# Streaming encoder step on one core: levels two and three of the triangular inverse by one product of 128 columns, token copies moved behind

## The chip, the cores and the metric

One Trainium2 chip, one core of it. The metric is the device time of one execution in microseconds, the median of several runs. Everything is computed in float32 (the large matrix products as a sum of three products of split operands).

## The reference, cut to what matters

The kernel does one inference step of a two-layer trunk on 512 prompt tokens and 64 sample tokens (576 columns together). In each layer a norm and an input projection feed two groups of token mixers; their outputs are projected back, and a convolutional feed-forward part follows. The change touches only the RWKV-7 mixer, whose reference is a scan over tokens:

```
def step(s, inp):
    rt, wt, kt, vt, at, bt = inp
    sa = jnp.einsum('bhvk,bhk->bhv', s, at)
    s = s * wt[:, :, None, :] + sa[..., None] * bt[:, :, None, :] + vt[..., None] * kt[:, :, None, :]
    y = jnp.einsum('bhvk,bhk->bhv', s, rt)
    return s, y
```

There are 8 heads with a 64 by 64 state each. The kernel does the scan in chunks of 64 tokens. Inside a chunk each token depends on the earlier ones through a strictly triangular 64 by 64 matrix L per head, and the kernel needs the inverse of (1 - L). It is built as a product, T = (1 + L)(1 + L^2)(1 + L^4)..., over five levels of squaring. The GLA mixer, a chunked linear attention, runs interleaved with it.

## The kernel before, in words

**Stages.** In each layer come the input projection (dense products, two weight tiles in flight), the chunk loop over nine chunks (one of sample tokens, eight of prompt tokens), the output projection, and two halves of the feed-forward part. `passes` (L643 to L652) issues the dense products. The chunk loop is written out by hand for every engine: each engine has one function per step and calls them in a fixed order in its own loop `for i in range(-1, LAST)`. Turn i of the loop finishes chunk i (state, outputs) and prepares chunk j = i + 1 (its masks, its inverse). Each step waits on semaphores whose counts are named by the lists `PE_F`, `AC_F`, `DV_F`, `PO_F`: `nth(AC_F, n, "L2A")` is the count reached when ScalarE has done that step of chunk n.

**The inverse.** The eight heads stand as two sets, A (`hp` 0) and B (`hp` 1), each with two X and, in each X, two heads on the two halves of the partitions. `DET` is a double buffer in SBUF with three slots of 64 columns for each set and X: slot 0 holds the power L^n, slot 1 the growing inverse T, slot 2 the transposed power. Level k reads buffer (k + 1) % 2 and its results go to buffer k % 2:

- TensorE, `level(j, hp, k)`: for each X and for both heads it multiplies slot 2 by slot 0 (L882: the next power, levels 1 to 3), slot 0 by slot 2 (L885: its transpose, levels 1 to 4), both into the PSUM bank `gr[hp]`, and slot 2 by slot 1 (L888: the product that T grows by, levels 2 to 5) into another PSUM bank, `tk[hp]`. The stationary operand of L882 and L888 is the same, slot 2.
- ScalarE, `copy_powers(j, hp, k)` (L1479, at level 4 L1481): copies the powers from `gr[hp]` to `DET`.
- VectorE, `add_power(j, X, k)` (L2057): adds the product in `tk` to T. It waits for the level on TensorE and for T of the level before. Level k + 1 on TensorE waits for both the copy and the addition.

The banks `tk` also hold, from column 0 to 383, the transposed tokens of the chunk (`tokens(j)`, L861), which ScalarE copies out in one instruction, `copy_tokens(j)` (L1471). So level 2 waits for this copy (name "tok" in `AC_F`). In the loop of ScalarE it stands ahead of the copies of level 1.

**Order around it on TensorE in turn i:** `carried` (L908), `solve_z` (L932), `carried_y` (L920), `gram` (L849, L851), `solve_z1` (L942), `gla_scores` (L997), means, `solve_z2` (L950), `tokens`, level 1 of A and of B, `solve_u` (L958), sums of squares (L670, L671) in some turns, level 2 A and B, `outputs` (L966 to L977), `gla_tokens` (L1006, L1008), level 3 A and B, `post_squares_y` (L670, L671) in some turns, `gla_out` (L1024, L1028), level 4 A and B, `gla_state` (L1038, products of 128 columns), level 5 A and B. In the first turn `turn_state` (L821) stands between level 4 and `gla_state`.

**ScalarE in turn i:** copies of carried terms (L1487, L1494), of Z1 (L1499), roots and mixed outputs of an earlier group in some turns (L1573, L1579, L1588, L1597), `copy_tokens`, the copies of level 1, U (L1499 again), statistics (L1555, L1527, and a logarithm, L1561, for turns with a GLA group), the copies of level 2, statistics, the GLA tokens (L1646), the copies of level 3, a logarithm (L1567) or mixed outputs, the GLA outputs (L1656), the copies of level 4.

**VectorE in turn i:** `add_z` (L2066), masks (L2034, L2036, L2043), `add_rest` (L2082), GLA scores (L2102), statistics and scalings (L2131, L2142, L2149, L2157, L2165, L2171), the additions of level 2, `new_state` (L2095, L2097), `add_y` (L2076), in some turns the low parts of the squares that `post_squares_y` sums (L2142), the additions of levels 3 and 4, `new_gla_state` (L2114, L2116), the additions of level 5.

Of the kernel before, what the change touches and what calls it, by code (L numbers as in the profile page):

```python
# [31 lines left out]
C = 64  # L32
# [76 lines left out]
AC_F = ["tok", "L1A", "L1B", "L2A", "L2B", "L3A", "L3B", "L4A", "L4B"]  # L109
# [31 lines left out]
def program(nc, x_prompt, x_sample, state_gla, state_rwkv, state_rwkv_shift, cache_ffn_conv,  # L141
# [4 lines left out]
    with ExitStack() as ctx:  # L146
# [187 lines left out]
        pe_f, ac_f, dv_f, po_f = sem("pe_f"), sem("ac_f"), sem("dv_f"), sem("po_f")  # L334
# [311 lines left out]
        def _(pe):  # L646
# [80 lines left out]
            for l in range(0, DEPTH):  # L727
# [137 lines left out]
                def level(j, hp, k):  # L865

                    N, d = "AB"[hp], DET[(k + 1) % 2]
                    powers = gr[hp][:, 0:4 * C].rearrange("p (x c t) -> p x c t", x=2, c=2)
                    product = pair3(tk[hp][:, 0:2 * C])
                    if k == 1:  # L870
                        front(dv_f, DV_F, j, "M" + N)
                    else:
                        front(ac_f, AC_F, j, f"L{k - 1}{N}")
                        if k == 2:
                            front(po_f, PO_F, j, "T" + N)
                            front(ac_f, AC_F, j, "tok")
                        else:
                            front(dv_f, DV_F, j, f"L{k - 1}{N}")
                    for X in range(2):
                        for h in HEADS:  # L880
                            if k < 4:
                                mm = e.matmul(powers[h, X, 0], d[h, hp, X, 2], d[h, hp, X, 0], start=True, stop=True)  # L882
                        for h in HEADS:
                            if k < 5:
                                mm = e.matmul(powers[h, X, 1], d[h, hp, X, 0], d[h, hp, X, 2], start=True, stop=True)  # L885
                        for h in HEADS:
                            if k > 1:
                                mm = e.matmul(product[h, X], d[h, hp, X, 2], d[h, hp, X, 1], start=True, stop=True)  # L888
                    mm.then_inc(pe_f, 1)
# [33 lines left out]
                def solve_z(i):  # L923

                    front(ac_f, AC_F, i, "tok")
                    front(dv_f, DV_F, i, "MB")
                    glas(ac_g, AC_G, i, "oE")
                    if i > 0:
                        back(dv_a, DV_A, i - 1, "Y")
                    for n, hp, X, o in solved(zb):  # L930
                        for h in HEADS:
                            mm = e.matmul(o[h], EK[i % 2][h, hp, X, 1, C:2 * C], tok[i % 2][h, X, 2, hp, :],  # L932
                                          start=True, stop=True)
                    mm.then_inc(pe_b, 2 if i == 1 else 1)
# [313 lines left out]
        def _(ac):  # L1248
# [87 lines left out]
            for l in range(0, DEPTH):  # L1336
# [131 lines left out]
                def copy_tokens(j):  # L1468
# [3 lines left out]
                                 PS[1].rearrange("p (x n) -> p x n", x=2)[:, :, 0:6 * C], ACT.Copy).then_inc(ac_f, 1)  # L1472

                def copy_powers(j, hp, k):

                    step(pe_f, PE_F, j, f"L{k}" + "AB"[hp])
                    src = gr[hp][:, 0:4 * C].rearrange("p (x c t) -> p x c t", x=2, c=2)
                    if k < 4:
                        e.activation(DET[k % 2][:, hp, :, 0:3:2, :], src, ACT.Copy).then_inc(ac_f, 1)  # L1479
                    else:  # L1480
                        e.activation(DET[k % 2][:, hp, :, 2, :], src[:, :, 1, :], ACT.Copy).then_inc(ac_f, 1)  # L1481
# [127 lines left out]
                for i in range(-1, LAST):  # L1609
# [18 lines left out]
                    copy_tokens(j)  # L1628
# [11 lines left out]
                    copy_powers(j, 1, 2)  # L1640
                    if i == LAST - 1:
# [6 lines left out]
                    copy_powers(j, 1, 3)  # L1648
                    if i == LAST - 1:
# [81 lines left out]
        def _(dv):  # L1731
# [30 lines left out]
            for l in range(0, DEPTH):  # L1762
# [284 lines left out]
                def add_power(j, X, k):  # L2047
# [7 lines left out]
                    src = pair3(tk[X][:, 0:2 * C])  # L2055
# [316 lines left out]
```

## Time and profile before

| what | value |
|---|---|
| median of 3 runs | 1640.76 us (1640.54 to 1641.64) |
| the profiled execution, its own time | 1642.36 us |
| its span, first to last instruction | 1640.6 us |
| granted TensorE clock, mean | 0.996 |
| TensorE busy with matmuls | 1610.7 us, 98% of the span |
| VectorE, ScalarE, GpSimd busy | 955.0, 681.9, 593.6 us |
| chunk loops with their tails | about 211 to 357 us and 1012 to 1157 us of the span |

In the profile one float32 matmul of the code stands as two MATMUL records (and two weight loads). A timeline row "x4" of L882 is therefore the two heads of one X. Such a row's start is when its first record began, and its length runs to the modelled end of its last one, so the rows of a busy TensorE overlap; the distance between starts tells what a piece of work occupies. "Idle before" counts only time in which no matmul record was open, which is less than the gap in starts.

### The profile page before, as it was taken

The page shows a single profiled execution, that of the slowest core. Times are in us where ns is not written, and L with a number is a line of the kernel's source. Part 1 is how long each engine was busy: PE and PEld are TensorE (multiplying, and loading weights), DVE is VectorE, ACT ScalarE, POOL GpSimd, SP SyncE. Part 2 cuts the span into 40 slices and gives each one's busy share as a digit, 9 for nine tenths or more (in the row PEclk, how much of TensorE's full clock was granted, in tenths as well). Part 3 has the DMA queues.
Part 4 walks back from the last instruction along what each step waited for, and adds up shares of the span by engine and source line. Part 5 has one row for each costly group of instructions (what it writes and reads, how often), then busy time and mean ns, then how long its engine had stood idle before and what let it go on. Part 6 is the DMA issues. An engine that isn't in the chain of part 4 may idle for free.

```text
span 1640.6 us, 40498 instructions
## 1 busy us (share of the span) xinstructions
PE 1610.7 (98%) x17981; PEld 1568.9 (96%) x17981; DVE 955.0 (58%) x1474; ACT 681.9 (42%) x1071; POOL 593.6 (36%) x345
## 2 busy tenths in 40 slices
PE   7999999999999999999999999999999999999997
PEld 6999989989999999999999999988999999999997
DVE  4579646666566305666537894566656660266643
ACT  5455356663433213333344644566443331233332
POOL 5345422123343434343334453131234343343431
PEclk9999999999999999999999999999999999999999
DMA  4222210002323322223232222000232232223331
GB/s 141 75 72 82 70 42 4 4 22 78 91 78 95 89 75 78 87 81 98 79 90 65 78 78 72 11 4 4 59 90 78 84 104 74 75 79 89 92 91 58
DMA packets 218863, 115.39 MB, mean 70 GB/s; under 512 B 9332, under 2 KB 216450, under 8 KB 218690
## 3 DMA queue, kind: packets, MB, share of 16 engines
q1 hardware_dynamic: 218610, 112.79, 24.3%
q8 instruction: 142, 2.33, 0.6%
q14 instruction: 31, 0.25, 0.0%
q10 hardware_dynamic: 80, 0.02, 0.0%
HBM read 109.27 MB, written 3.53 MB: 69 GB/s over the span
## 4 chain that ended last, share of the span: by engine, by line
PE 95%; ACT 2%; DVE 1%; issue 1%; DMA 0%; SPq 0%; DVEq 0%; ACTq 0%
PE ps L652 38%; PE ps L651 38%; PE ps L885 2%; PE ps L888 2%; PE ps L882 2%; PE ps L849 1%; PE ps L1024 1%; PE ps L656 1%; PE ps L781 1%; PE ps L1006 1%; PE ps L670 1%; PE ps L861 1%; PE ps L950 1%; PE ps L942 1%; PE ps L1163 0%
## 5 line engine op out<-in xcount | busy, mean ns | idle before, releaser
L547 POOL TENSOR_TENSOR wlo<-raw,whi 128x1024 fp32r<-128x1024 f32 (+1 forms) x186 | 503.0, 2704 | 758.1 <-ACT whi L1261 758.0
L1261 ACT ACTIVATE whi<-raw 128x1024 fp32r<-128x1024 f32 (+1 forms) x186 | 207.4, 1115 | 618.4 <-PE ps L652 618.4
L651 PE MATMUL ps<-xh,whi 128*128 128x288 f32 x1120 | 331.8, 296 | 4.5 <-DVE xl L1743 4.5
L652 PE MATMUL ps<-xh,whi 128*128 128x288 f32 x1120 | 331.5, 296 | 0.0
L651 PE MATMUL ps<-xl,whi 128*128 128x288 f32 x1120 | 330.5, 295 | 0.0
L652 PE MATMUL ps<-xl,whi 128*128 128x288 f32 x1120 | 329.1, 294 | 0.0
L652 PE MATMUL ps<-xh,wlo 128*128 128x288 f32 x1120 | 328.9, 294 | 0.0
L651 PE MATMUL ps<-xh,wlo 128*128 128x288 f32 x1120 | 328.9, 294 | 0.0
L651 PEld LDWEIGHTS ps<-xh,whi 128*128 128x128 f32 x1120 | 210.7, 188 | 6.9 <-issue 4.5
L652 PEld LDWEIGHTS ps<-xh,whi 128*128 128x128 f32 x1120 | 210.8, 188 | 0.2
L651 PEld LDWEIGHTS ps<-xh,wlo 128*128 128x128 f32 x1120 | 210.9, 188 | 0.0
L652 PEld LDWEIGHTS ps<-xl,whi 128*128 128x128 f32 x1120 | 210.8, 188 | 0.0
L651 PEld LDWEIGHTS ps<-xl,whi 128*128 128x128 f32 x1120 | 210.3, 188 | 0.0
L652 PEld LDWEIGHTS ps<-xh,wlo 128*128 128x128 f32 x1120 | 210.1, 188 | 0.0
L2280 DVE TENSOR_TENSOR x<-x,ps 128x576 f32<-128x576 f32 x48 | 36.2, 754 | 192.0 <-PE ps L652 189.4
L2318 DVE SCALAR_TENSOR_TENSOR cv<-up,par,cv 128x578 f32<-128x578 f32 x44 | 100.5, 2283 | 32.8 <-ACT cv L1699 32.8
L2333 DVE SCALAR_TENSOR_TENSOR hl<-hf,hh 128x576 fp32r<-128x576 f32 x44 | 98.4, 2237 | 33.3 <-ACT hh L1705 33.3
L652 PE MATMUL ps<-hh,whi 128*128 128x288 f32 x352 | 103.7, 295 | 0.0
L652 PE MATMUL ps<-hl,whi 128*128 128x288 f32 x352 | 103.6, 294 | 0.0
L651 PE MATMUL ps<-hl,whi 128*128 128x288 f32 x352 | 103.5, 294 | 0.0
L651 PE MATMUL ps<-hh,wlo 128*128 128x288 f32 x352 | 103.4, 294 | 0.0
L651 PE MATMUL ps<-hh,whi 128*128 128x288 f32 x352 | 103.4, 294 | 0.0
(330 smaller groups left out, 3202.4 us busy)
## 6 DMA issues: line engine op xcount, KB each, us to landing
raw<-in_ffn_w_up SPq DMA_DIRECT2D x88, 512.0 KB, 3.8
raw<-in_w_in SPq DMA_DIRECT2D x52, 512.0 KB, 3.7
raw<-in_ffn_w_down SPq DMA_DIRECT2D x32, 704.0 KB, 4.6
raw<-in_w_out SPq DMA_DIRECT2D x16, 512.0 KB, 4.0
xin<-in_x_prompt SPq DMA_DIRECT2D x4, 512.0 KB, 6.5
out<-xin SPq DMA_DIRECT2D x8, 256.0 KB, 2.9
out<-RW SPq DMA_DIRECT2D x16, 64.0 KB, 2.2
g<-in_rwkv_g SPq DMA_DIRECT2D x2, 256.0 KB, 2.9
```

The costliest lines, as they stand in the source:

```text
L547: e.tensor_tensor(wlo[s][:, 0:width], raw[s][:, 0:width], whi[s][:, 0:width].bitcast(F32), ALU.subtract).then_inc(w_lo[s], 1)
L651: e.matmul(acc(out)[:, 0], lhsT, rhs[:, 0:HT], start=start, stop=stop)
L652: return e.matmul(acc(out)[:, 1], lhsT, rhs[:, HT:TOK], start=start, stop=stop)
L656: e.matmul(out[:, 0:512], lhsT, rhs[:, 0:512], start=True, stop=True)
L670: e.matmul(out, weights[:, :], rest_hi[b][:, 0:n // 2], start=True, stop=False)
L882: mm = e.matmul(powers[h, X, 0], d[h, hp, X, 2], d[h, hp, X, 0], start=True, stop=True)
L885: mm = e.matmul(powers[h, X, 1], d[h, hp, X, 0], d[h, hp, X, 2], start=True, stop=True)
L888: mm = e.matmul(product[h, X], d[h, hp, X, 2], d[h, hp, X, 1], start=True, stop=True)
L1261: e.activation(whi[s][:, 0:width], raw[s][:, 0:width], ACT.Copy).then_inc(w_hi[s], 1)
L2280: e.tensor_tensor(by_half(xt), by_half(xt), acc(PS[s]), ALU.add).then_inc(psum_free[s], 1)
L2318: e.scalar_tensor_tensor(out=cv[:, :], in0=up[:, 1:3 + TOK], scalar=par[:, cw + FF + f:cw + FF + f + 1], in1=cv[:, :], op0=ALU.mult, op1=A ...
L2333: e.scalar_tensor_tensor(out=hl[:, it, :], in0=hf[:, :], scalar=1.0, in1=hh[:, it, :].bitcast(F32), op0=ALU.mult, op1=ALU.subtract).then_i ...
```

## The change

- At levels 2 and 3 the next power and the product for T come from one matmul of 128 columns: the stationary operand is slot 2, the moving one slots 0 and 1 together. Both results and the transposed power go to the bank `gr[hp]`, in three slots per X. At level 4 the product for T goes to `gr[hp]` too; at level 5 it still goes to `tk[hp]`.
- VectorE's addition reads `gr[hp]` at levels 2 to 4. It now waits also for ScalarE's copy of the same level and set, since both read the same bank.
- Level 2 no longer waits for the token copy. Level 5 does, by a semaphore of its own (`ac_t`), and so does `solve_z`.
- `copy_tokens(j)` moves on ScalarE from ahead of the copies of level 1 to behind the copies of level 2, in turns with a group of RWKV statistics (i of 2, 4, 6, 7) to behind those of level 3.
- Within a level the transposed power (L885) is now issued before the other product.

```
-AC_F = ["tok", "L1A", "L1B", "L2A", "L2B", "L3A", "L3B", "L4A", "L4B"]
+AC_F = ["L1A", "L1B", "L2A", "L2B", "L3A", "L3B", "L4A", "L4B"]
+AC_T = ["tok"]
...
-                    powers = gr[hp][:, 0:4 * C].rearrange("p (x c t) -> p x c t", x=2, c=2)
-                    product = pair3(tk[hp][:, 0:2 * C])
+                    out = gr[hp][:, 0:6 * C].rearrange("p (x c t) -> p x c t", x=2, c=3)
...
                         if k == 2:
                             front(po_f, PO_F, j, "T" + N)
-                            front(ac_f, AC_F, j, "tok")
                         else:
+                            if k == 5:
+                                front(ac_t, AC_T, j, "tok")
                             front(dv_f, DV_F, j, f"L{k - 1}{N}")
                     for X in range(2):
-                        for h in HEADS:
-                            if k < 4:
-                                mm = e.matmul(powers[h, X, 0], d[h, hp, X, 2], d[h, hp, X, 0], start=True, stop=True)
+                        first, last = int(k > 3), 1 if k == 1 else 2
                         for h in HEADS:
                             if k < 5:
-                                mm = e.matmul(powers[h, X, 1], d[h, hp, X, 0], d[h, hp, X, 2], start=True, stop=True)
+                                mm = e.matmul(out[h, X, 2], d[h, hp, X, 0], d[h, hp, X, 2], start=True, stop=True)
                         for h in HEADS:
-                            if k > 1:
-                                mm = e.matmul(product[h, X], d[h, hp, X, 2], d[h, hp, X, 1], start=True, stop=True)
+                            to = out[h, X, first:last] if k < 5 else pair3(tk[hp][:, 0:2 * C])[h, X]
+                            mm = e.matmul(to, d[h, hp, X, 2], d[h, hp, X, first:last], start=True, stop=True)
                     mm.then_inc(pe_f, 1)
...
-                    src = gr[hp][:, 0:4 * C].rearrange("p (x c t) -> p x c t", x=2, c=2)
+                    src = gr[hp][:, 0:6 * C].rearrange("p (x c t) -> p x c t", x=2, c=3)
                     if k < 4:
-                        e.activation(DET[k % 2][:, hp, :, 0:3:2, :], src, ACT.Copy).then_inc(ac_f, 1)
+                        e.activation(DET[k % 2][:, hp, :, 0:3:2, :], src[:, :, 0:3:2, :], ACT.Copy).then_inc(ac_f, 1)
...
-                    copy_tokens(j)
                     copy_powers(j, 0, 1)
                     copy_powers(j, 1, 1)
...
                     copy_powers(j, 0, 2)
                     copy_powers(j, 1, 2)
+                    if py is None:
+                        copy_tokens(j)
...
                     copy_powers(j, 0, 3)
                     copy_powers(j, 1, 3)
+                    if py is not None:
+                        copy_tokens(j)
...
-                    src = pair3(tk[X][:, 0:2 * C])
+                    if k < 5:
+                        step(ac_f, AC_F, j, f"L{k}{N}")
+                    src = gr[X][:, 0:6 * C].rearrange("p (x c t) -> p x c t", x=2, c=3)[:, :, 1, :] if k < 5 else \
+                        pair3(tk[X][:, 0:2 * C])
```

## Rows read from the trace of the kernel before

**Rows 1.** The page's first part, TensorE's line: busy us (share of the span) x instructions.

```profile
PE 1610.7 (98%) x17981; PEld 1568.9 (96%) x17981; DVE 955.0 (58%) x1474; ACT 681.9 (42%) x1071; POOL 593.6 (36%) x345
```

**Rows 2.** Busy time by stretch, the first chunk loop: us, then each engine, clock, DMA.

```profile
211.00:357.00 146.00, 141.73 (x3974) 129.58 (x3973) 89.88 (x239) 92.72 (x215) 27.20 (x44) 1.00 0.05 13
```

**Rows 3.** Groups by line, L882: tile, shape, count | busy, mean ns | idle before.

```profile
L882 PE MATMUL ps<-work 64*64 64x64 f32 x864 | 60.4, 222 | 1.2 <-ACT work L1479 1.2
```

**Rows 4.** Timeline of TensorE, solve_u (L958) and level 2 in three chunks: start, length.

```profile
240.19 0.63 PE L958 MATMUL ps<-work 64*64 64x64 f32 x16
240.65 0.28 PE L882 MATMUL ps<-work 64*64 64x64 f32 x4
...
270.18 0.63 PE L958 MATMUL ps<-work 64*64 64x64 f32 x16
271.00 0.33 PE L882 MATMUL ps<-work 64*64 64x64 f32 x4 [0.19 <-ACT work L1479]
...
301.01 0.63 PE L958 MATMUL ps<-work 64*64 64x64 f32 x16
302.04 0.33 PE L882 MATMUL ps<-work 64*64 64x64 f32 x4 [0.40 <-ACT work L1479]
302.21 0.28 PE L885 MATMUL ps<-work 64*64 64x64 f32 x4
```

**Rows 5.** Timeline of ScalarE in the third of these chunks.

```profile
300.93 0.79 ACT L1471 ACTIVATE work<-ps 128x768 f32<-128x768 f32 x1
301.62 0.65 ACT L1479 ACTIVATE work<-ps 128x256 f32<-128x256 f32 x2
```

**Rows 6.** Timeline of TensorE: level 3, first and last row; gla_state (L1038); level 5.

```profile
289.74 0.28 PE L882 MATMUL ps<-work 64*64 64x64 f32 x4
...
291.02 0.28 PE L888 MATMUL ps<-work 64*64 64x64 f32 x4
...
293.92 0.60 PE L1038 MATMUL ps<-work 64*64 64x128 f32 x8
294.36 0.56 PE L888 MATMUL ps<-work 64*64 64x64 f32 x13
```

**Rows 7.** The same time, ScalarE's and VectorE's level 4; then one hand-over between them.

```profile
293.67 0.28 ACT L1481 ACTIVATE work<-ps 128x128 f32<-128x128 f32 x1 [0.17 <-PE ps L888]
294.14 0.28 ACT L1481 ACTIVATE work<-ps 128x128 f32<-128x128 f32 x1 [0.19 <-PE ps L888]
...
293.67 0.29 DVE L2057 TENSOR_TENSOR work<-work,ps 128x128 f32<-128x128 f32 x1 [2.03 <-PE ps L888]
294.14 0.29 DVE L2057 TENSOR_TENSOR work<-work,ps 128x128 f32<-128x128 f32 x1 [0.18 <-PE ps L888]
...
299.87 0.63 ACT L1573 ACTIVATE work<-work 128x512 f32<-128x512 f32 x1
...
300.53 1.12 DVE L2149 SCALAR_TENSOR_TENSOR G<-G,par,work 128x512 f32<-128x512 f32 x1 [0.33 <-ACT work L1573]
```

**Rows 8.** Timeline of a turn with RWKV statistics: ScalarE, VectorE, TensorE.

```profile
288.46 0.65 ACT L1479 ACTIVATE work<-ps 128x256 f32<-128x256 f32 x2
...
289.02 0.42 DVE L2095 TENSOR_TENSOR work<-work,ps 128x256 f32<-128x256 f32 x1 [0.68 <-PE ps L977]
290.15 0.75 DVE L2142 TENSOR_TENSOR wlo<-work,whi 128x256 fp32r<-128x256 f32 x2
...
291.24 0.38 PE L670 MATMUL ps<-whi,mean64r 128*128 128x256 f32 x1
```

**Rows 9.** Timeline of the last chunk and the tail behind it: ScalarE, VectorE, TensorE.

```profile
341.70 0.43 ACT L1481 ACTIVATE work<-ps 128x128 f32<-128x128 f32 x2
...
341.88 0.68 DVE L2165 TENSOR_TENSOR ml<-G,mh 128x512 fp32r<-128x512 f32 x1
344.50 0.42 DVE L2066 TENSOR_TENSOR work<-work,ps 128x256 f32<-128x256 f32 x1
...
344.97 0.68 PE L942 MATMUL ps<-work 64*64 64x64 f32 x16 [0.34 <-DVE work L2066]
```

More of the change, by code:

```diff
@@ L333, in program @@
         st_dve = sem("st_dve")
-        pe_f, ac_f, dv_f, po_f = sem("pe_f"), sem("ac_f"), sem("dv_f"), sem("po_f")
+        pe_f, ac_f, ac_t, dv_f, po_f = sem("pe_f"), sem("ac_f"), sem("ac_t"), sem("dv_f"), sem("po_f")
         pe_b, ac_b, dv_b, dv_a = sem("pe_b"), sem("ac_b"), sem("dv_b"), sem("dv_a")
@@ L923, in solve_z @@
                 def solve_z(i):
-                    front(ac_f, AC_F, i, "tok")
+                    front(ac_t, AC_T, i, "tok")
                     front(dv_f, DV_F, i, "MB")
@@ L1471, in copy_tokens @@
                     e.activation(tok[j % 2].rearrange("p x a h t -> p x (a h t)"),
-                                 PS[1].rearrange("p (x n) -> p x n", x=2)[:, :, 0:6 * C], ACT.Copy).then_inc(ac_f, 1)
+                                 PS[1].rearrange("p (x n) -> p x n", x=2)[:, :, 0:6 * C], ACT.Copy).then_inc(ac_t, 1)
                 def copy_powers(j, hp, k):
                     step(pe_f, PE_F, j, f"L{k}" + "AB"[hp])
-                    src = gr[hp][:, 0:4 * C].rearrange("p (x c t) -> p x c t", x=2, c=2)
+                    src = gr[hp][:, 0:6 * C].rearrange("p (x c t) -> p x c t", x=2, c=3)
                     if k < 4:
-                        e.activation(DET[k % 2][:, hp, :, 0:3:2, :], src, ACT.Copy).then_inc(ac_f, 1)
+                        e.activation(DET[k % 2][:, hp, :, 0:3:2, :], src[:, :, 0:3:2, :], ACT.Copy).then_inc(ac_f, 1)
                     else:
-                        e.activation(DET[k % 2][:, hp, :, 2, :], src[:, :, 1, :], ACT.Copy).then_inc(ac_f, 1)
+                        e.activation(DET[k % 2][:, hp, :, 2, :], src[:, :, 2, :], ACT.Copy).then_inc(ac_f, 1)
                 def copy_carried(i):
```

## The prediction, made before the changed kernel was run

> **What bounds the kernel now.** I read the page first, then the stretches, the timelines of the chunk loop, and the groups. The page says that TensorE has matmuls open 98% of the span [rows 1], and that holds inside the chunk loop too: 141.73 of 146 us at full clock [rows 2]. So what counts is the distance between starts of successive TensorE work. The reader is to see two things there. First, TensorE is paced by its own stream nearly everywhere, so fewer or cheaper matmuls pay at once. Second, the few stalls are hand-overs of some tenths of a us: 2A (level 2 of set A) in two chunks of each layer starts late, behind ScalarE's copy of level 1 [rows 4]; and level 5 starts just after level 4 has been copied and added [rows 6, 7]. The change works on both, with opposite signs. The loop has 9 chunks in each of 2 layers, 18 in all.
>
> **Part 1, the wide products.** A pair (both heads of an X) of 64 columns: level 3 has twelve, and from the start of the first, 289.74, to that of the last, 291.02, are eleven of them, so 1.28/11 = 0.1165 us each [rows 6]. Levels 2 and 3 have 6 such pairs per set, of which 2 are L882 and 2 are L888. These four become two pairs of 128 columns. The nearest row is `gla_state`, with the same 64*64 tiles, the same two heads and 128 columns: 2 pairs in 294.36 - 293.92 = 0.44 us, 0.22 each [rows 6]. Two narrow pairs cost 0.233, the wide one 0.22: 0.013 us saved. Merged pairs: 2 X x 2 sets x 2 levels x 18 = 144, so 1.9 us. All of it lies on TensorE's stream, hence on the path. Of L882's 864 records [rows 3] those of levels 2 and 3, 576, go; but the columns they streamed stay, and at 64 columns the columns already are the cost. Bounds: nothing saved; or, were all cost per matmul and none per column, 0.117 x 144 = 16.8 us, which the wide row excludes since it took 0.22 and not 0.117. I take the row.
>
> The Trainium skill, "TensorEngine Tiling (Array Packing)", section "Instruction Overhead", says that each matmul carries some 60 cycles of overhead. That rule speaks for far more than this row; here the distance grows from 0.117 to 0.22 when the columns double, so only 0.013 us of it is fixed, and the trace disagrees. The time by that rule is the third rival.
>
> **Part 2, the token copy moved behind.** Undisturbed, 2A starts 240.65 - 240.19 = 0.46 us after `solve_u`; in two other chunks it starts 0.82 and 1.03 us after it [rows 4]. There ScalarE did the token copy from 300.93 and reached level 1's copies only at 301.62, though level 1A had been over for a us [rows 5]. Without it the copy of 1A starts at 300.93 and ends at 301.31, before TensorE is through with `solve_u`. Both stalls go: 0.36 + 0.57 = 0.93 us a layer, 1.9 in all; the second layer shows the same two. Other turns have no stall of this kind at 2A; the first chunk's wait is PE to copy to PE with no token copy in between. Below: nothing, if another producer (GpSimd's start of T, U) were as late; neither is due then. What is late next: nothing before level 3.
>
> At its new place the copy (0.79 us) needs ScalarE behind level 2's or 3's copies. Turns without RWKV statistics leave over a us idle before the GLA tokens. In the others it pushes a logarithm or mixed outputs into the wait for `gla_out`. It costs nothing, and its readers (level 5, next turn's `solve_z`) come over a us later. No DMA and no GpSimd or SP queue is passed. The copies of the powers keep their sizes (256 and 128 columns), so they keep their durations; so do additions.
>
> **Part 3, the addition now behind the copy.** Today the copy and the addition of level 4 run side by side: both start at 293.67 for A and at 294.14 for B [rows 7]. They become a chain. Where does TensorE come back soon? Between levels 2 and 3 and between 3 and 4 it has about a us or more of other work, which covers a chain longer by 0.32 us. Between 4 and 5 there is only `gla_state`, 0.44 us:
> - 5A: the copy ends 293.95; the addition starts 0.03 later (ScalarE ended at 299.87 + 0.63 = 300.50, VectorE started 300.53 [rows 7]), takes 0.29 and ends at 294.27; TensorE starts 0.05 after VectorE (344.50 + 0.42 = 344.92, then 344.97 [rows 9]), at 294.32. It comes at 294.36 anyway [rows 6]: no loss, with 0.04 to spare.
> - 5B: the copy ends 294.42, the addition runs 294.45 to 294.74, TensorE could start at 294.79. Today it is due at 294.36 + 2 pairs x 0.117 = 294.59. A stall of 0.20. After a stall the first pair takes 302.21 - 302.04 = 0.17 and not 0.117 [rows 4], so 0.05 more: 0.25, say 0.24.
>
> Chunks 2 to 8 of each layer have this pattern to the hundredth; in the first, `turn_state` stands in between and covers it. So 14 x 0.24 = 3.4 us. Bounds: nothing if hand-overs overlap wholly, and 14 x 0.35 = 4.9 if 5A slips past its 0.04 too. I take 3.4.
>
> **Part 4, what queues behind the waiting addition on VectorE.** (a) In turns with statistics ScalarE does level 2's copies late, 288.46 to 289.11 [rows 8]. VectorE then adds 2B only at about 289.14 to 289.43, so `new_state`, 289.02 today, starts near 289.35, 0.33 later. The low parts of the squares behind it end at 290.90 + 0.33 = 291.23, and L670, due at 291.24 less 0.11 saved, waits for them and a 0.05 hand-over: 0.15 us. Two turns a layer are so; the first such turn copies earlier. 4 x 0.15 = 0.6 us. Bounds 0 and 1.3 (0.33 each). (b) In the last chunk the level 4 copies run 341.70 to 342.13; VectorE's additions follow and release L2165 at about 342.41, not 341.88 [rows 9]. VectorE is solid from there to `add_z`, at 344.50 today because of another wait; it slips some 0.3, and L942, which already waits for it, with it. 2 x 0.3 = 0.6 us. Bounds 0 and 1.0.
>
> **The sum.** -1.9 - 1.9 + 3.4 + 0.6 + 0.6 = +0.8 us. The profiled execution's own time is 1642.36 us (span 1640.6), 1.6 above the median of 1640.76; it would become 1643.2. Against the median: 1641.6 us. Expected gain and new wait cancel. A measurement of this kernel can tell about 0.2%, 3.3 us, from no change.
>
> **The rivals.**
> - **The hand-over also misses at 5A** (slower). Place: level 5 of set A. It has 0.04 us of slack in 14 chunks. If ScalarE to VectorE to TensorE takes 0.1 longer than the two rows used, each of the two links feels it: 5A starts 0.1 late, 5B 0.35 to 0.45 late, and in turns with statistics 0.25. Price: 14 x 0.42 + 4 x 0.25 + 1.0 = 7.9, less 3.8: +4.1, 1644.9 us. For it: VectorE must also pass two semaphore waits. Against: the two rows show quick links. It decides from 0.04 us. Chance 0.16.
> - **The wide product saves nothing** (the change doesn't do what it says): its pair takes 0.233. +1.9 on the sum: 1643.5 us. For it: a third slot per X spreads the writes. Against: `gla_state`. Chance 0.08.
> - **A fixed cost per matmul weighs more than `gla_state` shows** (faster). If it were 0.05 us a merged pair, 144 x 0.05 = 7.2 saved in place of 1.9, -4.5: 1636.3 us. The size is that of the page's 60 cycles, two records at 2.4 GHz; this is an estimate. Rows 6 speak against it. Chance 0.04.
> - **The new stall is covered** (at the edge of faster). If level 5B's weights are ready and its wait ends early, at half the price, and part 4 vanishes: -3.8 + 1.7 = -2.1, 1638.7 us. For it: 5B today overlaps with `carried` behind it. Against: `carried` stands behind 5B in one queue. Chance 0.12, a third of it below -0.2%.
>
> **How the numbers follow.** My forecast, 1641.6, has the remaining 0.60. Most of the rest lies within 3.3 us of no change. Faster by over 0.2% (under 1637.5) takes the third rival, part of the fourth and some room for what I overlook: 0.10. Slower (over 1644.0) takes most of the first, part of the second and the upper bounds: 0.17. Same: 0.73. The range from 1638.0 to 1645.0 takes in the fourth rival and the first and leaves out under 2 in 10.
>
> **What would show it.** L882 and L888 of levels 2 and 3 as one line of 64x128 with 576 records, starts 0.22 apart per pair; a level 2 of both sets in 1.35 us, not 1.40. 2A 0.46 after `solve_u` in every turn without sums. In the waits, a new row: TensorE's product of level 5 behind L2057 of VectorE, about 14 times 0.05 to 0.2. L2057 of level 4 starting at the end of L1481, not with it. L670 waiting for L2142 in two more turns a layer. The dense stages unchanged to 0.1 us. Wrong would be: 5B starting on time (then faster), 5A late as well (slower), or a wide pair off 0.22.

## The result, and the profile after

| | before | changed |
|---|---|---|
| median of 6 runs on one chip | 1640.37 us | 1646.44 us (1645.59 to 1648.53) |
| the profiled execution, own time and span | 1642.36, 1640.6 us [rows 1] | 1648.53, 1646.8 us |

The ratio is 1.0041 [1.003, 1.0051]: slower by 6.1 us, past my bound for "same" and outside my range. Profiled execution against profiled execution it is 6.2 us. Of all executions below one, of the first experiment, took 2136.9 us at a granted clock of 0.69, and it is left out of its ratio. The page of the changed kernel, its span and the engines' busy times:

```profile
span 1646.8 us, 39346 instructions
...
PE 1613.6 (98%) x17405; PEld 1564.6 (95%) x17405; DVE 955.0 (58%) x1474; ACT 683.2 (41%) x1071; POOL 592.7 (36%) x345
```

The 576 records of the merged products are gone (17981 less 17405 [rows 1]), yet TensorE is open 2.9 us longer: 98% busy hides stalls of tenths. The stretches of the changed kernel (columns as in [rows 2]) are both chunk loops with their tails, and all between them:

```profile
211.00:357.00 146.00, 140.59 (x3672) 125.54 (x3672) 88.19 (x234) 91.18 (x212) 27.62 (x45) 1.00 0.05 13
357.00:1012.00 655.00, 655.00 (x4944) 647.05 (x4946) 383.24 (x493) 239.64 (x308) 261.28 (x104) 1.00 0.29 81
1012.00:1160.00 148.00, 140.94 (x3714) 125.97 (x3707) 89.26 (x237) 92.55 (x214) 29.70 (x45) 1.00 0.06 14
```

The clock is full in both loops, and in between TensorE never lacks an open record. The loss is in the loops and behind them, at full clock. TensorE's waits in the changed kernel (us in total, times, longest):

```profile
PE ps L671 <- DVE wlo L2147: 2.3, 6, 0.6
PE ps L949 <- ACT work L1498: 2.0, 8, 0.3
...
PE ps L941 <- issue: 1.9, 3, 0.8
PE ps L887 <- DVE work L2062: 1.2, 3, 0.5
```

The line numbers have moved: L887 is the product (wide or narrow) that was L882 and L888, L884 the transposed power, L1478/L1480 the copies of powers, L2062 the addition, L671 the sums of squares, L2147 their low parts. These four rows hold 7.4 us of waits, but the view counts only time in which no record was open. The stalls of level 5 hardly appear in it: its 1.2 us are three waits, in the 14th chunk and the two last ones. Distances between starts show the others. TensorE of the changed kernel, the turn of [rows 6]:

```profile
291.60 0.39 PE L887 MATMUL ps<-work 64*64 64x128 f32 x4
291.82 0.28 PE L884 MATMUL ps<-work 64*64 64x64 f32 x4
...
292.60 0.36 PE L671 MATMUL ps<-whi,mean64r 128*128 128x256 f32 x1 [0.28 <-DVE wlo L2147]
...
295.14 0.28 PE L887 MATMUL ps<-work 64*64 64x64 f32 x4
295.26 0.61 PE L1037 MATMUL ps<-work 64*64 64x128 f32 x8
295.85 0.82 PE L887 MATMUL ps<-work 64*64 64x64 f32 x13
296.46 0.27 PE L907 MATMUL ps<-work,RW 64*64 64x64 f32 x2
```

The wide pair takes 291.82 - 291.60 = 0.22, as forecast. But from `gla_state` to level 5 it is 0.59 (295.26 to 295.85), where before it was 0.44 [rows 6]: 5A is late too, by 0.15. 5B is another 0.19 late behind 5A. The chain behind it, ScalarE and VectorE of the same turn:

```profile
295.01 0.28 ACT L1480 ACTIVATE work<-ps 128x128 f32<-128x128 f32 x1 [0.17 <-PE ps L887]
295.47 0.28 ACT L1480 ACTIVATE work<-ps 128x128 f32<-128x128 f32 x1 [0.19 <-PE ps L887]
...
295.42 0.29 DVE L2062 TENSOR_TENSOR work<-work,ps 128x128 f32<-128x128 f32 x1 [2.25 <-ACT work L1480]
295.88 0.29 DVE L2062 TENSOR_TENSOR work<-work,ps 128x128 f32<-128x128 f32 x1 [0.18 <-ACT work L1480]
```

Copy and addition, side by side in [rows 7], are a chain now, as said. Its links are longer than I took: the copy is over at 295.29 and the addition starts at 295.42, **0.13** later; the addition is over at 295.71 and level 5 starts at 295.85, **0.14 to 0.15** later. I had 0.03 and 0.05.

By chunk, over the 18 chunks (distance from the start of the last record ahead to that of the level's first): 5A went from 0.10 to 0.25 and 5B from 0.05 to 0.24 in 13 of the 14 chunks. In the 14th, chunk 2 of layer two, 5A stands at 0.60 and 5B at 0.02. In the last chunk of each layer 5A went from 0.20 to 0.72. L671 behind level 3 went from 0.15 to 0.54 in four turns (0.05 of it is the longer last record). In the other direction, 2A is on time in all chunks (four late ones of 0.41 or 0.62 are 0.05 now). Both sets of level 3 together take 1.24 from first to last start, for 1.35, of which the next start gives back 0.05: 0.06 a level, 2.1 us over 36 levels.

The 14th chunk, ScalarE, then VectorE:

```profile
1036.38 0.28 ACT L1480 ACTIVATE work<-ps 128x128 f32<-128x128 f32 x1 [0.17 <-PE ps L887]
...
1037.14 0.48 DVE L2062 TENSOR_TENSOR work<-work,ps 128x128 f32<-128x128 f32 x2 [1.16 <-ACT work L1480]
```

The addition starts 0.48 behind the copy and not 0.13. VectorE's last wait ahead of it ended at 1036.74; elsewhere the addition starts 0.05 after that, here 0.40. The kernel before with the added wait alone has the same 0.40 in the same chunk. What holds VectorE there is open.

2A in a turn with a root and mixed outputs ahead of it, TensorE, then ScalarE (that of [rows 5]):

```profile
302.47 0.63 PE L957 MATMUL ps<-work 64*64 64x64 f32 x16
302.93 0.28 PE L884 MATMUL ps<-work 64*64 64x64 f32 x4
...
302.38 0.68 ACT L1478 ACTIVATE work<-ps 128x256 f32<-128x256 f32 x2
```

The start stands 0.46 behind `solve_u`, where it stood 1.03 [rows 4]. The ledger, from level 1A of a layer's first chunk to that of its last: both loops went from 239.78 to 244.74 us. From layer one's last chunk to layer two's first it took 680.84 for 680.49, and from layer two's last chunk to TensorE's last product 502.06 for 501.65; these 0.35 and 0.41 are the tails. The first chunk began 0.53 later. Of the loops' 4.96, 1.86 belongs to nothing in the change: gaps inside one function's products with no releaser, 0.74 us in sum before, 2.60 after. I call them pauses. One of them, TensorE in `solve_z1`:

```profile
313.26 0.51 PE L941 MATMUL ps<-work 64*64 64x64 f32 x11
314.53 0.38 PE L941 MATMUL ps<-work 64*64 64x64 f32 x5 [0.76 <-issue]
```

Eleven records, then nothing for 0.76 us, then the other five of the same step. So **loops less pauses** is what I compare from here: 239.04 before, 242.14 changed, +3.1.

### The profile page after: what moved, and what is told of

Its sections match the earlier page's. It is cut to its first block, busy times and chain, and to the rows that moved or that the text cites. A ratio compares the mean times of both kernels' runs of the same rounds, so it can differ in the third digit from the quotient of the medians.

```text
span 1646.8 us, 39346 instructions
## 1 busy us (share of the span) xinstructions
PE 1613.6 (98%) x17405; PEld 1564.6 (95%) x17405; DVE 955.0 (58%) x1474; ACT 683.2 (41%) x1071; POOL 592.7 (36%) x345
## 4 chain that ended last, share of the span: by engine, by line
PE 95%; ACT 2%; DVE 1%; issue 1%; DMA 1%; SPq 0%; DVEq 0%; ACTq 0%
PE ps L653 38%; PE ps L652 38%; PE ps L887 3%; PE ps L884 2%; PE ps L850 1%; PE ps L862 1%; PE ps L949 1%; PE ps L1023 1%; PE ps L657 1%; PE ps L782 1%; PE ps L941 1%; PE ps L957 1%; DMA xin<-in_x_prompt 1%; PE ps L931 0%; PE ps L1162 0%
```

## The experiments

There are two theories on the loops' 3.1. **First theory:** the loss is the chain copy, addition, TensorE, each link 0.1 longer than I took, because the late wait rides on an instruction of its own; the wide products and the moved copy save what I said. **The rival** in each run puts the loss in the other part that the run touches (the wide products, the copy's new place, the number of waits and not their order). Two more on the pauses: they come from where the instruction stream lies, or from the code around them. "The changed kernel" below is its profiled execution. For the ratios, the kernel before was run beside each of four groups of experiments, 21 or 22 times each (medians 1640.08, 1640.05, 1639.91 and 1639.72, on three chips).

**Level 4's product back in its own bank** (so without the wait at level 4; levels 2 and 3 as changed, the token copy then needed by level 4).

```
-                            if k == 5:
+                            if k == 4:
                                 front(ac_t, AC_T, j, "tok")
...
-to = out[h, X, first:last] if k < 5 else pair3(...)
+to = out[h, X, first:last] if k < 4 else pair3(...)
...
-                    if k < 5:
+                    if k < 4:
                         step(ac_f, AC_F, j, f"L{k}{N}")
```

> The changed kernel, but level 4's product for T goes to the tk bank again, so its addition runs beside the copy. Theory 1 (the chain copy, addition, TensorE at level 5 costs 0.15 at set A and 0.24 at set B in 14 chunks): 5A starts 0.10 us after gla_state's last record and 5B 0.05 after 5A, as in the kernel before; 5.5 us go, and 0.3 to 0.6 in the two tails: about 1640.5 us where the changed kernel has 1646.4. Theory 2 (the loss comes from elsewhere, such as stalls without a releaser in the z1 solve, and level 5 merely shows it): level 5 is on time and the time stays above 1644.

1639.39 us, 0.9997 [0.9988, 1.0006]: 7.0 below the changed kernel. Loops less pauses 236.46, 5.7 less than changed. Both starts of level 5 are back at 0.10 and 0.05:

```profile
290.86 0.61 PE L1037 MATMUL ps<-work 64*64 64x128 f32 x8
291.30 0.56 PE L887 MATMUL ps<-work 64*64 64x64 f32 x13
```

0.44 again, where the changed kernel had 0.59. L671 stays late (2.3 us in six waits, as changed), since its cause stands at level 2. So the wait at level 4 costs 5.7 us in the loops, more than their whole loss.

**The wide product split into two of 64 columns**, all else as changed.

```
-                            to = out[h, X, first:last] if k < 5 else pair3(tk[hp][:, 0:2 * C])[h, X]
-                            mm = e.matmul(to, d[h, hp, X, 2], d[h, hp, X, first:last], start=True, stop=True)
+                            if k < 4:
+                                mm = e.matmul(out[h, X, 0], d[h, hp, X, 2], d[h, hp, X, 0], start=True, stop=True)
+                        for h in HEADS:
+                            if k > 1:
+                                to = out[h, X, 1] if k < 5 else pair3(tk[hp][:, 0:2 * C])[h, X]
+                                mm = e.matmul(to, d[h, hp, X, 2], d[h, hp, X, 1], start=True, stop=True)
```

> The changed kernel with the 128-column product of levels 2 and 3 split into two of 64 columns into the same bank; every wait is kept. Theory 1 (a wide pair takes 0.22 us, two narrow ones 0.233): 144 x 0.013 = 1.9 us slower than the changed kernel, about 1648.3. Theory 2 (the wide product saves nothing): 1646.4. Theory 3 (a fixed cost of 0.05 per merged pair): 1653.6.

1647.83 us, 1.0045 [1.0032, 1.0058]; loops less pauses 243.77, 1.63 above changed, where I had 1.9. Levels 2 and 3 take their old time again, 0.06 a level and 2.1 us in all; 0.5 of it comes back because L671, in its four turns, has 0.12 us less to wait. The wide product saves, and little.

**The token copy ahead of level 1's copies again.** The edit is the two moves of the change in `copy_tokens`, undone.

> The changed kernel with the token copy ahead of level 1's copies again. Theory 1 (moving it saved the two stalls at level 2A in each layer, 0.36 and 0.57): they come back, 1.9 us slower than the changed kernel, 1648.3. Theory 2 (the time was only moved to the next wait, so it was no gain): 1646.4, with the stalls at 2A and as much less elsewhere.

1647.11 us, 1.0042 [1.0028, 1.0055]; loops less pauses 244.22, +2.08. The late 2A of 0.41 and 0.62 return in the same four chunks. That part of the change is worth 2 us, as forecast.

**One wait for one** (VectorE waits for the copy alone at levels 2 to 4, which implies the level; TensorE at levels 3 to 5 for the addition alone, which implies the copy).

```
-                        front(ac_f, AC_F, j, f"L{k - 1}{N}")
                         if k == 2:
+                            front(ac_f, AC_F, j, f"L{k - 1}{N}")
                             front(po_f, PO_F, j, "T" + N)
                         else:
+                            front(dv_f, DV_F, j, f"L{k - 1}{N}")
                             if k == 5:
                                 front(ac_t, AC_T, j, "tok")
-                            front(dv_f, DV_F, j, f"L{k - 1}{N}")
...
-                    step(pe_f, PE_F, j, f"L{k}{N}")
+                    if k < 5:
+                        step(ac_f, AC_F, j, f"L{k}{N}")
+                    else:
+                        step(pe_f, PE_F, j, f"L{k}{N}")
...
-                    if k < 5:
-                        step(ac_f, AC_F, j, f"L{k}{N}")
```

> The changed kernel with one wait in each link of the chain: the addition of levels 2 to 4 waits for the copy alone (it implies the level on TensorE), TensorE's levels 3 to 5 for the addition alone. The same order of work. Theory 1 (a hand-over takes 0.13 to 0.15 us in the changed kernel because the wait that ends last is not the one the instruction itself carries; carried by it, 0.03 to 0.05): VectorE starts within 0.05 of the copy's end, 5A is back at 0.10, 5B still 0.2 late; 14 x 0.15 + 4 x 0.15 = 2.7 less, about 1643.7 us. Theory 2 (the hand-over costs as much whatever carries the wait): 1646.4, with the gaps unchanged.

1639.93 us, 1.0002 [0.9993, 1.001]; loops less pauses 238.17, 4.0 below changed, more than I expected. 5A is on time (0.10), 5B stands at 0.24, L671 at 0.44 and not 0.54. The chain is as long in instructions as before this edit. Only its links are shorter.

**The same waits, named in another order**: the late one first (VectorE: copy, then level; TensorE: addition, then copy). No wait added or taken away.

```
+                        if k > 2:
+                            front(dv_f, DV_F, j, f"L{k - 1}{N}")
                         front(ac_f, AC_F, j, f"L{k - 1}{N}")
...
-                        else:
-                            if k == 5:
-                                front(ac_t, AC_T, j, "tok")
-                            front(dv_f, DV_F, j, f"L{k - 1}{N}")
+                        if k == 5:
+                            front(ac_t, AC_T, j, "tok")
...
+                    if k < 5:
+                        step(ac_f, AC_F, j, f"L{k}{N}")
                     step(pe_f, PE_F, j, f"L{k}{N}")
...
-                    if k < 5:
-                        step(ac_f, AC_F, j, f"L{k}{N}")
```

> The changed kernel with all its waits, only the order in which they are named changed: the copy's first in VectorE's addition, the addition's first in TensorE's levels 3 to 5. Theory 1 (the instruction carries the wait named first, the others go ahead of it as instructions of their own, and the late one costs 0.1 us more there): the same gaps as with one wait, 5A back at 0.10 and VectorE within 0.05 of the copy's end, 2.9 us less than the changed kernel, 1643.5. Theory 2 (it was the number of waits that cost): gaps as in the changed kernel, 1646.4.

1641.15 us, 1.0008 [0.9999, 1.0017]; loops less pauses 238.41, 3.7 below changed and 0.2 from one wait. Level 4 to 5 in this kernel: ScalarE, VectorE, TensorE:

```profile
290.81 0.28 ACT L1480 ACTIVATE work<-ps 128x128 f32<-128x128 f32 x1 [0.17 <-PE ps L887]
...
291.12 0.29 DVE L2062 TENSOR_TENSOR work<-work,ps 128x128 f32<-128x128 f32 x1 [2.14 <-ACT work L1480]
...
291.06 0.60 PE L1037 MATMUL ps<-work 64*64 64x128 f32 x8
291.50 0.81 PE L887 MATMUL ps<-work 64*64 64x64 f32 x13
```

From 291.09 to 291.12 is 0.03, the value of my sum, and level 5A comes 0.44 behind `gla_state`. So the order of naming costs 3.7 us in the loops, the number of waits next to nothing. The records show why: an instruction carries the wait named first, and the others stand ahead of it as a semaphore instruction of their own. In the changed kernel the wait for the copy stands in VectorE's semaphore instruction, which ends at 295.37, 0.09 after the copy, and the addition starts 0.05 later. With the copy named first the addition itself carries that wait, and nothing late stands ahead of it. On TensorE the same shows at 5B: its product starts 0.05 behind the end of B's addition (291.88 to 291.93), where the changed kernel has 0.15 (296.17 to 296.32).

**The added wait alone**: the kernel before, with only the wait of the addition for the copy, at levels 2 to 4. Nothing is merged or moved.

```
                         step(dv_f, DV_F, j, f"L{k - 1}{N}")
+                    if k < 5:
+                        step(ac_f, AC_F, j, f"L{k}{N}")
```

> The kernel before with one line more: VectorE's addition of levels 2 to 4 also waits for ScalarE's copy of that level and set. No wide product, no token copy moved, no bank changed. Theory 1 (this wait is what costs): level 5A 0.15 and 5B 0.24 late in 14 chunks, L670 up to 0.35 late in 4, the tails 0.4 each: 5.5 + 1.4 + 0.8 = 7.7 us slower than the kernel before, about 1647.8. Theory 2 (a large part of the changed kernel's loss is in the wide products or the moved copy): under 1644.

1649.57 us, 1.0055 [1.0042, 1.0068]: +9.7. Loops less pauses +6.36. 5A stands at 0.25 and 5B at 0.24 as in the changed kernel, 5A at 0.60 in the same one chunk and at 0.72 in the last chunks. The wait by itself gives more than the whole loss, and the rest of the change wins 3 us back.

**The logarithm behind level 2's copies** (`log_o` moved behind the copies and the rounding, to free L671).

> The changed kernel with ScalarE's logarithm of the GLA squares (and the table load ahead of it) behind level 2's copies and the rounding of the squares, not ahead of them. Theory 1 (in turns with RWKV statistics the late copies of level 2 hold VectorE's additions, and with them new_state and the low parts that L671 waits for, 0.35 us in 4 chunks): L671 comes 0.20 after level 3 and not 0.54, 1.4 us less, about 1645.0. Theory 2 (L671 is then held by the logarithm instead, or gla_out by the later token copy): 1646.4 or more, with a new gap there.

1645.3 us, 1.003 [1.0019, 1.0042]; loops less pauses 241.38, -0.76. L671 is on time in all four turns (0.35 each, 1.4 us), but in chunk 2 of each layer, where no RWKV statistics follow, the logarithm now delays the GLA outputs by 0.18 and level 4 by 0.19 (0.7 us). Only half of the edit pays. It also shows that the late copy of level 2, and not the addition's length, held L671.

**All of it together**: level 4 apart, one wait (VectorE's at levels 2 and 3; TensorE's stay as changed), late logarithm.

> Level 4's product apart in tk, the logarithm late, and the addition of levels 2 and 3 waiting for the copy alone: the wide products and the moved token copy with none of the three losses found. Theory 1 (the two gains are whole): 1640.1 - 1.9 - 1.9 = 1636.3 us. Theory 2 (one of them is given back further on): 1638 to 1640, as with level 4 apart alone.

1639.66 us, 0.9996 [0.9987, 1.0005]. Loops less pauses 235.96, 3.1 less than before; but 3.10 us of pauses, where before has 0.74, eat most of it.

**The same with the late logarithm only in turns with RWKV statistics.**

> As the combination run before (level 4 apart, additions of levels 2 and 3 waiting for the copy alone), but with the logarithm late only in turns with RWKV statistics. With the logarithm late in the first full turn too, gla_out came 0.18 late and level 4 0.19; this goes. Theory 1: chunk loops 0.7 us shorter than in the combination, no stall at L671 nor before gla_out, and about 1639 or, with fewer pauses of the instruction stream, down to 1636.5. Theory 2 (a new wait replaces it): as the combination, 1639.7.

1638.54 us, 0.9994 [0.9985, 1.0003]; loops less pauses 235.24, 3.8 less than before, pauses 3.15. The time stays above what the loops promise.

**The pauses.** First the changed kernel once more, unedited.

> The changed kernel itself once more, for the pauses of 0.3 to 1.0 us inside one line's matmuls that no engine releases: its first profile has five in the chunk loops (in gram at 281 us, in the z1 solve at 235, 314, 1084 and 1134 us or so, 2.7 us together), the kernel before three smaller ones (0.8 us). Theory 1 (they belong to where the instruction stream stands in memory): the same places and sizes again, and some 2 of the 6 us slower are theirs. Theory 2 (chance): other places, another sum. The time stays near 1646.4.

1645.78 us, 1.0035 [1.0022, 1.0047]; loops less pauses 242.15 (242.14), pauses 2.19 (2.60). TensorE of this second execution:

```profile
309.44 0.51 PE L941 MATMUL ps<-work 64*64 64x64 f32 x11
310.72 0.38 PE L941 MATMUL ps<-work 64*64 64x64 f32 x5 [0.76 <-issue]
```

The same record of the same chunk as above, and as long. The largest three lie in the same chunks in both. So a pause has a place in the stream. Then the stream was shifted: 32 transposes at the very start, into a bank that is written anew before anyone reads it (their results are used nowhere; nothing of the computation is left out).

```
             pe.wait_ge(gains_loaded, 48)
+            for _ in range(32):
+                e.transpose(PS[3][:, 0:(2 * DEPTH + 1) * KT], rows_g[:, :], ident[...])
```

> The changed kernel with 32 more small transposes of the same rows on TensorE at its very start, where it waits for the inputs: 64 more matmul records and as many weight loads, so that everything behind stands that much further on in TensorE's instruction stream; the chunk loops are untouched. Both profiles of the changed kernel have pauses in the z1 solve of the same three chunks (0.98 and 0.98, 0.83 and 1.15, 0.77 and 0.27 us). Theory 1 (a pause belongs to the place in the stream where the next piece of instructions has to be fetched): they leave these chunks and turn up in others, and the sum of 2.2 to 2.6 us changes. Theory 2 (they belong to the work at that place): the same three chunks again. Time 1644 to 1647; the start may cost up to 2 us more.

1647.15 us, 1.0035 [1.0022, 1.0049]. The three long pauses are gone, and the loops took 241.82 us for 244.74; but the first chunk starts at 213.85 and not 211.94, since these transposes stand in the way. One new pause stands where the changed kernel has none:

```profile
1117.01 0.38 PE L671 MATMUL ps<-whi,mean64r 128*128 128x256 f32 x1
1117.53 0.39 PE L672 MATMUL ps<-wlo,mean64r 128*128 128x256 f32 x1
```

These starts are 0.52 apart and not 0.22 as in the changed kernel, and up to the next function 0.4 us go. The waits don't list it, since the first record's length leaves less than 0.15 us idle. With it loops less pauses are 241.4. The code in the loop is the same and the pauses are others: their place comes from the stream.

The same in the last combination:

> best2 with the same 32 transposes at the start. Theory 1 (pauses belong to places in the instruction stream): another set of pauses, and a time that differs from best2's by the difference of the pauses in the two profiles, up to 2 us either way. Theory 2: the same time and the same chunks.

1640.42 us, 0.9999 [0.999, 1.0008]: pauses 1.41 for 3.15, and a start at 214.63 for 212.33. To shift without that cost, the transposes (of the identity, again unused) were put ahead of the first wait for an input, where TensorE is idle, with 8, 16 and 24 of them (here 16).

```
             pe.wait_ge(consts, N_IDENT)
+            for _ in range(16):
+                e.transpose(PS[3][:, 0:P], ident[:, :], ident[:, :])
             pe.wait_ge(gains_loaded, 48)
```

> best2 with 8 idle transposes of the identity on TensorE before its first wait for an input, in time in which it has nothing to do: the instruction stream behind stands 32 instructions further on, and nothing else changes. Theory 1 (the pauses of the instruction stream, 3.2 us in best2's loops, hide its gain): the pauses change in place and sum, and the time follows them: 1636.5 with under 1 us of pauses, 1639 with 3. Theory 2 (the pauses don't set the time): 1638.5 whatever they are.

> As before with 16 transposes, 64 instructions. Theory 1: another set of pauses, the time by their sum, 1636.5 to 1639. Theory 2: 1638.5.

> As before with 24 transposes, 96 instructions. Theory 1: another set of pauses, the time by their sum, 1636.5 to 1639. Theory 2: 1638.5.

| transposes | median, us | ratio | both loops | pauses seen | loops less pauses | first chunk starts |
|---|---|---|---|---|---|---|
| 0 | 1638.54 | 0.9994 [0.9985, 1.0003] | 238.40 | 3.15 | 235.24 | 212.33 |
| 8 | 1637.89 | 0.9985 [0.9976, 0.9994] | 236.84 | 1.85 | 234.99 | 209.23 |
| 16 | 1637.96 | 0.9991 [0.9982, 1.0] | 235.75 | 0.54 | 235.20 | 212.07 |
| 24 | 1635.3 (1634.64 to 1636.09) | 0.9971 [0.9959, 0.9982] | 235.47 | 1.38 | 234.09 | 208.42 |

With 24 it beats both kernels: 4.4 us below the kernel before, 11 below the changed one. The loops are the same code four times, yet loops less pauses spread over 1.15 us, in part because I counted only gaps inside one function. With 16 transposes the largest stands between two:

```profile
250.49 0.66 PE L943 MATMUL ps<-work 64*64 64x64 f32 x16
251.90 0.45 PE L998 MATMUL ps<-G 64*64 64x64 f32 x8 [0.75 <-issue]
```

In starts it is 0.92 us; with it 16 transposes have 1.46 us of pauses, and 234.28 without them. With 8 there is one more such gap, of 0.30. So a difference of loops less pauses under about 1 us says nothing by itself, the 0.76 of the late logarithm among them; there the distances between starts speak.

The profiled executions with 0 and with 24 transposes span 1641.1 and 1634.4 us: 3.9 of the 6.7 lie in the start and 2.9 in the loops. The medians are only 3.2 apart. Between 16 and 24 the loops differ by 0.27 and the medians by 2.7, so the loops alone don't sort the table. The start differs too. The first 40 us of the profiled execution with 16 and then with 24 transposes (columns as in [rows 2]):

```profile
0.00:20.00 20.00, 12.20 (x69) 10.73 (x69) 8.89 (x9) 14.33 (x21) 15.26 (x51) 0.82 0.70 209
20.00:40.00 20.00, 19.09 (x141) 17.21 (x141) 9.74 (x25) 7.56 (x12) 4.29 (x3) 0.84 0.21 56
```

```profile
0.00:20.00 20.00, 13.69 (x84) 12.78 (x85) 10.05 (x12) 15.24 (x23) 15.60 (x51) 0.91 0.69 210
20.00:40.00 20.00, 19.31 (x161) 17.55 (x161) 9.11 (x22) 6.31 (x10) 7.06 (x3) 1.00 0.33 87
```

At a granted clock of 0.84 against 1.00, 141 and not 161 records fit in the same 20 us, and the first chunk starts 3.65 us later. The means hide a step. With 16 transposes it lies here:

```profile
26.07 0.44 PE L653 MATMUL ps<-xh,whi 128*128 128x288 f32 x1
26.31 0.42 PE L652 MATMUL ps<-xl,whi 128*128 128x288 f32 x1
...
26.83 0.29 PE L653 MATMUL ps<-xh,wlo 128*128 128x288 f32 x1
26.96 0.29 PE L652 MATMUL ps<-xh,whi 128*128 128x288 f32 x1
```

The products start 0.24 us apart until then, at the lower of the clock's two levels (1.2 GHz, a granted 0.50), and 0.13 apart behind it, at the upper (2.4 GHz). With 24 transposes the same step comes at 19.7 us. Before it TensorE had waited over 3 us for VectorE and had then run dense products again. That isn't a matter of the kernel alone: the changed kernel's two profiled executions began their chunks at 211.94 and 208.54, with 0.86 and 1.00 in that stretch. Whether the 24 transposes move the step, or these executions happened to have it early, no run here tells. The profile without transposes reads 1.00 throughout, though its products too start 0.24 apart up to 26.1 us: here the starts are the better witness.

## Why the prediction was wrong

By its own steps:

- **Part 1, the wide products: right.** 0.22 a pair, and 2.1 us for my 1.9 by the starts of levels 2 and 3; splitting them again cost 1.6 in the loops, since 0.5 came back at L671. The 16.8 that a cost per matmul would have given is excluded.
- **Part 2, the token copy: right** in place and size: four late starts, 1.9 us by their starts, 2.08 when put back. Nothing else is late for its new place.
- **Part 3, the addition behind the copy: this step failed**, in the sentence "TensorE starts 0.05 after VectorE ... at 294.32. It comes at 294.36 anyway: no loss, with 0.04 to spare". The chain was right, its two hand-overs weren't. I took 0.03 and 0.05 from rows in which the late wait was the only one or named first, so that the waiting instruction carried it. In the change, both waits are the last named. They measured 0.13 and 0.15, which is 0.2 more. With 0.04 to spare, 5A is late by 0.15. 5B comes 0.19 late behind that, and the two levels, each restarted, take 0.07 longer themselves (0.46 for 0.39). 14 chunks of 0.41, one of them 0.53, are 5.8 us and not 3.4; putting level 4 apart gave back 5.7. My first rival said just this ("each of the two links feels it") and its price, 1644.9, was too small only by the pauses; I gave it 0.16 where two rows of another kind of wait were all that spoke against it.
- **Part 4: the place right, the size low.** (a) L671: 0.15 to 0.54, less 0.05 of the longer record, is 0.34 a turn and not 0.15, in four turns: 1.4 for 0.6. One wait for one took 0.10 of it back, so that much is the two links; the late logarithm took back all, so the rest is ScalarE's late copies, which the additions now wait for. (b) The tails: 0.35 and 0.41 against 0.3. In them 5A comes 0.52 later, but L942 waited there anyway.
- **The sum.** In the loops -2.1, -1.9, +5.8 and +1.4 give +3.2, where the trace has 3.1; with 0.76 in the tails, some +3.9. Pauses add 1.86 in one profiled execution and 1.45 in the other: 5.3 to 5.7. Measured 6.1 and 5.7.
- **Left out of the sum: the pauses.** No row of before warned that they would grow; they were there, though, at 0.74 us, as gaps without a releaser.

Shown by runs: that the added wait alone makes the loss, that the order of naming makes 3.7 us of it, that both savings are real, that the pauses move with the stream. That a pause is the time of a late piece of the instruction stream is borne out by the traces, though no run held a piece back. The queue that fetches the stream, in the changed kernel's page and in that of the kernel before:

```profile
q8 instruction: 138, 2.26, 0.6%
```

```profile
q8 instruction: 142, 2.33, 0.6%
```

That's 16 KB a piece, and in the changed kernel's loops one every 4.7 us. The pause at 314.53 ends 1.43 us after such a piece landed (it was under way from 311.74 to 313.10). Over both loops of all 17 profiled executions there are 56 pauses of 0.2 us or more (three of them between two functions), and every one ends 1.2 to 1.6 us after a piece landed; of all of TensorE's records only 8% start in that stretch behind a piece. Yet of the 52 pieces in the changed kernel's loops only four have a pause behind them. Why just these is open, as is how many of the 1.5 to 1.9 us the median of many runs holds.

That the addition must wait at all comes from the bank: both engines read `gr[hp]` now. The Trainium skill, "PSUM — Partial Sum Buffer", on bank collisions, says that ScalarE and VectorE may not read one bank in the same quadrant at once. No run here tried it without the wait. What it costs where the product stays in a bank of its own is shown: nothing.

## What to carry to other kernels

When a change puts a wait in a chain, take the price of the hand-over from a row in which the late wait stands where it will stand in the new code. Name the wait that comes last first, and leave out those that it implies; here that was worth 3.7 to 4.0 us with no work moved. A result that two engines need soon should go to two banks where the next step has only tenths of a microsecond of cover, even if one bank would spare the wider product; and a loop of small products should be judged by its starts less its pauses, those between two functions too, before the time is put down to an edit.

## What the runs showed of the hardware that I had not expected

- **Order of waits.** ScalarE to VectorE 0.03 and VectorE to TensorE 0.05 us with the late wait named first, 0.13 and 0.15 with it named after another.
- **Pauses.** 0.2 to 1.3 us with no releaser in dense runs of small matmuls, 0.4 to 3.3 us of both loops; at the same record in two executions of one program, gone or elsewhere when 8 to 32 transposes are put ahead; all 56 of 0.2 us or more end 1.2 to 1.6 us after a 16 KB piece of the instruction queue landed.
- **Columns, not instructions.** On 64*64 tiles in float32, a pair of 64 columns takes 0.1165 us and one of 128 takes 0.22: 0.013 is fixed, and 0.015 a merged pair is what levels 2 and 3 gained.
- **The start and the end.** TensorE's step from the lower to the upper clock level came at 19.7 us in one execution and at 26.6 in another, of nearly the same kernel, and the first chunk 3.65 us later. In the changed kernel's two executions the stretch from L1234 to TensorE's last product took 5.4 us at a granted 0.72 and 6.8 us at 0.52.
